# Expert stage of a two-block decoder: the low part of the turned features moved ahead of one weight split

## The reference

```
logits = einsum('nd,de->ne', xt, router_w)
top_val, top_idx = top_k(logits, 2);  gates = softmax(top_val)
for every expert e, on the tokens that chose it:
    y = (silu(xb @ w1[e]) * (xb @ w3[e])) @ w2[e]
out[token] = sum over its two experts of gate * y
```

## Time and profile before

| | |
|---|---|
| time, median of 3 runs | 1962.66 us (1957.55 to 1963.01) |
| the profiled execution's own time | 1963.32 us |
| its span in the profile | 1961.6 us |
| PE busy | 1884.5 us (96%) |
| PE weight loads busy | 1616.9 us (82%) |
| DVE busy | 1542.4 us (79%) |
| ACT busy | 1196.6 us (61%) |
| transfers | 528.39 MB, 269 GB/s over the span |

### The profile page before, as it was taken

The page is one execution under the profiler, slowest core; times in us unless marked ns, Lnnn a source line. Parts: engine busy times, 40 slices in busy tenths (PEclk is TensorE's granted clock), DMA queues, the critical chain, the costliest instruction groups (busy, mean ns, idle before and its releaser), DMA issues.

```text
span 1961.6 us, 27157 instructions
## 1 busy us (share of the span) xinstructions
PE 1884.5 (96%) x10640; PEld 1616.9 (82%) x10640; DVE 1542.4 (79%) x2105; ACT 1196.6 (61%) x1642; POOL 51.3 (3%) x56
## 2 busy tenths in 40 slices
PE   7999999999999999999999999899899989989998
PEld 7889998777878887878787878688789978878997
DVE  5768887567999999999999999558588985856565
ACT  4544344544787888888888887556554446754443
POOL 0010000002000000000000010000000000000000
PEclk9999999999999999999999999999999999999999
DMA  7348886744999999999999999443268974324551
GB/s 311 129 161 308 336 343 248 278 161 156 414 379 377 383 367 380 373 375 367 385 367 388 366 396 360 173 151 108 87 236 331 356 288 151 108 86 166 189 193 44
DMA packets 75901, 528.39 MB, mean 269 GB/s; under 512 B 8658, under 2 KB 9042, under 8 KB 14322
## 3 DMA queue, kind: packets, MB, share of 16 engines
q1 hardware_dynamic: 69536, 504.40, 67.5%
q10 hardware_dynamic: 3060, 11.02, 1.5%
q0 software_dynamic: 3168, 11.14, 1.5%
HBM read 515.90 MB, written 11.01 MB: 269 GB/s over the span
## 4 chain that ended last, share of the span: by engine, by line
PE 87%; DVE 6%; ACT 4%; issue 2%; POOL 1%; DMA 0%; POOLq 0%; ACTq 0%; DVEq 0%
PE ps L554 27%; PE ps L556 26%; PE ps L555 26%; DVE w_lo L1396 2%; PE ps L775 2%; ACT w_hi L2304 1%; PE ps L727 1%; PE ps L740 1%; PE ps L990 1%; POOL stat L2815 1%; ACT xT L2314 0%; PE ps L818 0%; ACT score L2425 0%; ACT y_slots L2608 0%; DMA resid<-in_x 0%
## 5 line engine op out<-in xcount | busy, mean ns | idle before, releaser
L2304 ACT ACTIVATE w_hi<-ring 128x1024 fp32r<-128x1024 f32 x862 | 912.2, 1061 | 603.1 <-PE ps L556 594.7
L1396 DVE TENSOR_TENSOR w_lo<-ring,w_hi 128x1024 fp32r<-128x1024 f32 x862 | 1048.7, 1225 | 284.8 <-ACT w_hi L2304 251.4
L554 PE MATMUL ps<-w_hi,x_hi 128*128 128x512 f32 (+1 forms) x1056 | 410.8, 391 | 8.8 <-DVE w_lo L1396 3.6
L556 PE MATMUL ps<-w_hi,x_lo 128*128 128x512 f32 (+1 forms) x1056 | 400.1, 381 | 0.0
L555 PE MATMUL ps<-w_lo,x_hi 128*128 128x512 f32 (+1 forms) x1056 | 399.1, 380 | 0.0
L554 PE MATMUL ps<-x_hi,w_hi 128*128 128x256 f32 x1248 | 359.6, 288 | 4.6 <-DVE x_lo L1511 3.9
L555 PE MATMUL ps<-x_lo,w_hi 128*128 128x256 f32 x1248 | 355.4, 285 | 0.0
L556 PE MATMUL ps<-x_hi,w_lo 128*128 128x256 f32 x1248 | 355.2, 285 | 0.0
L554 PE MATMUL ps<-w_hi,h_hi 128*128 128x512 f32 x732 | 292.5, 400 | 2.7 <-DVE h_lo L2028 2.6
L555 PE MATMUL ps<-w_lo,h_hi 128*128 128x512 f32 x732 | 285.5, 390 | 0.0
L556 PE MATMUL ps<-w_hi,h_lo 128*128 128x512 f32 x732 | 284.9, 389 | 0.0
(11 more groups left out here) (298 smaller groups left out, 1327.4 us busy)
## 6 DMA issues: line engine op xcount, KB each, us to landing
ring<-in_stream SPq DMA_DIRECT2D x479, 1024.0 KB, 6.6
x_store<-arena ACTq DMA_DIRECT2D x1, 4096.0 KB, 27.5
arena<-x_store POOLq DMA_DIRECT2D x7, 512.0 KB, 8.0
y_store<-y_slots POOLq DMA_DIRECT2D x7, 512.0 KB, 8.9
con<-in_consts ACTq DMA_DIRECT2D x1, 2048.0 KB, 21.4
arena<-in_ln_rows ACTq DMA_DIRECT2D x3, 512.0 KB, 4.3
resid<-in_x SPq DMA_DIRECT2D x1, 1024.0 KB, 6.2
arena<-in_c ACTq DMA_DIRECT2D x2, 512.0 KB, 3.9
```

Of the source, the lines that this page charges most:

```text
L554: pe.matmul(out_, lhs[0], rhs[0], start=start, stop=False)
L556: return pe.matmul(out_, lhs[1], rhs[0], start=False, stop=stop)
L1396: dve.tensor_tensor(lo, ring[:, q % RING, a:a + HALF], hi.bitcast(F32), ALU.subtract)\
L2304: act.activation(half_buffer(m)[0], ring[:, q % RING, a:a + HALF], ACT.Copy).then_inc(hi_ready, 1)
```

## The change

In the order of DVE, `moe_lo` now stands one split earlier in every step s >= 1, as it did in the 11 steps named above. The splits and `moe_lo` are the same instructions with the same waits; ACT, PE, SP and GpSimd have the same programs as before.

```diff
@@ moe_step of the vector engine
                 e, j = s // J1, s % J1
                 n = up_slot(s)
                 if s >= 1:
-                    if j == 9 or (e == NE - 1 and j in (6, 7, 8)):
-                        split_to(reach(2 * n + 1))
-                    else:
-                        split_to(reach(2 * (n + 1)))
+                    split_to(reach(2 * n + 1))
                     moe_lo(s - 1)
                     split_to(reach(2 * (n + 1)))
                 split_to(reach(2 * (n + 2)))
```

## The result

The changed kernel takes 1948.62 us in the median of six runs (1947.48 to 1952.59), the kernel before 1963.01 (1957.55 to 1963.22), six runs beside it. The ratio is 0.9939, 95% interval 0.9928 to 0.995. The profiled execution took 1949.06 us with a span of 1947.3; before it was 1963.32 with 1961.6. Behind line 2052 all lines of the changed kernel lie three lower, so `w_hi` is L2301 and `h_hi` L2596.

The account below looks back on a forecast made before the run. PE was taken as the bound, its weight loads waiting for `h_lo`; 7.1 us (ordinary steps), 3.1 (second steps) and 0.8 (very first) sum to 11.0, taking 1963.32 to 1952.3, by the median 1951.7; predicted 1952, range 1945 to 1960.

Parts of the forecast that it names:

- two large terms: PE's wait for `h_lo` goes: 60 ordinary steps give 7.1 us, seven later second steps (j = 1) 3.1 us.
- the floor: Step length without the wait, 8.44 us, read from a tenth step that already had the new order.
- The alternative by matmul starts: Ordinary steps priced by the up-to-down matmul seam only: 0.54 - 0.45 = 0.09 us each, 5.4 us in all.
- The second term: Seven second steps (j = 1) of the later experts: 0.89 - 0.45 = 0.44 us each, 3.1 us in all.
- The margin at the low part: In step 44 the moved `h_lo` would end 0.9 us before PE needs it.
- D1's split costs nothing: D1's split on DVE comes about 0.7 us later in ordinary steps, with 1.1 us to spare before PE wants it.
- The plug (slower): Rival: DVE holds ready splits behind `h_lo` waiting for `h_hi`, in 76 steps; +17 us, 1980; chance 0.05.
- its point of decision: The plug decides when DVE idles over 0.9 us ahead of `h_lo`, that is, `h_hi` 0.5 us later.
- The transfers: Rival: transfers hold the expert stage, ordinary steps keep their length; only 3.9 us gained, 1959.4; chance 0.11.
- The cover of some 12.5 us: SP's ring: time left from slot issue to ACT's copy, against landings of 7.1 us median, 12.2 at most.

Follow-up runs that it names:

- e2: The changed kernel with the old order left in the second steps (j = 1): 1954.7 us, ratio 0.997.
- e1: The changed kernel with the old order left in the ordinary steps: 1958.11 us, ratio 0.9992.
- e3: The changed kernel with the low part one split earlier still, ahead of D0 and D1: 1986.89 us, ratio 1.014.
- e5: The changed kernel with three linked extra copies by ACT ahead of the real high part, delaying `h_hi`: 1994.81 us, one run.
- e4: The changed kernel with one linked extra copy by ACT ahead of the real high part, delaying `h_hi`: 1954.46 us, ratio 0.9962.
- e6: The changed kernel with slot refills in the expert stage held back until one more slot is split: 1947.7 us, one run.
- e7: The changed kernel with slot refills in the expert stage held back until two more slots are split: 1957.59 us, one run.

## Why the prediction was right

**The size and its two large terms.** For the stage 11.0 us was predicted, 12.0 came, and the experiments split it as the sum did: 7.8 (e2) for the ordinary steps where 7.1 stood, 4.2 (e1) for the second and first steps where 3.9 stood. The small shortfall of the first is the floor: it was read from one tenth step, 8.44, and the freed steps take 8.426, so 0.132 each and not 0.118. The alternative by matmul starts (0.09) would have missed 2.4 us: the whole step was the right measure, since the seam of the two matmuls shows only a part of what the step loses. The second term is by the windows 8.91 - 8.41 = 0.50 rather than 0.44, times seven, and 9.31 - 8.48 = 0.83 for the very first step against the 0.8 taken; these 4.3 agree with e1's 4.2.

**The margin at the low part** was mis-sized, without harm to the sum. "0.9 us before PE needs it" counted to the matmul; the wait stands at the load of its weights and costs from about 0.20 earlier, so the change has 2.79 - 2.04 = 0.75. The same omission made the expectations of e3 and e5 too mild. Neither the prediction nor the change asked whether that wait has to stand there.

**D1's split costs nothing:** shown, 1.17 us to spare up to the matmul where 1.1 was worked out (some 0.2 less up to the load of its weights), and the U1 split back behind ACT.

**The plug (slower).** Rightly given little, but its point of decision was only half understood. The prediction had DVE's idle time decide, from 0.9 us, or `h_hi` 0.5 us later. e4 lies below that (`h_lo` starts 2.05 behind the turn instead of 1.62, 0.76 idle) and is free, e5 and e3 lie above (1.38 and 1.28) and lose. The sum 7.55 + 1.38 = 8.93 even gives e5's step, but that is bookkeeping: DVE's idle time is then all ahead of `h_lo`. What PE waits for there is the low part, and the end of `h_lo` explains the losses of before too, where DVE didn't idle ahead of it at all. By the table the point lies some 0.7 us later (2.79 - 2.04 = 0.75), not 0.5. In e3 D0's split doesn't pass the waiting `h_lo`, though ACT's copy for it is done when `h_lo` starts at 859.25. That agrees with the Trainium skill, "TensorE: Matmul & The Clock Gate", section on the array's architectural detail, which has VectorE work strictly first in, first out. The order tells what is held up, not that it costs: in the changed kernel 0.41 us of waiting a step were free, in e3 0.45 of loss came when a split that PE wants earlier stood behind it.

**The transfers.** The rival falls: 383 GB/s in the ordinary steps of after at the share that gave 377, 409 in the second step. SP's waits and the landing, 470 to 1215 us, changed little against the earlier trace rows:

```profile
SPq L526 <- DVE w_lo L1396: 651.7, 261, 5.1
```

```profile
DMA to landing us min/median/max: 4.8/7.4/12.7
```

The cover of some 12.5 us was right enough for its purpose: e6 takes 2.8 of it at no cost, e7 5.6, and pays. That agrees with a landing of 7.4 in the median and up to 12.7.

**The time as a whole** lies 3.4 us under 1952. 1.0 of that is the stage. The rest is where the runs happen to lie, so that part of the agreement is luck; the range had been made wide for that. In the two profiled executions it is the clock ahead of the stage, and for the other runs no trace shows it.

## What to carry to other kernels

Measure a stage from turn to turn (or any start that repeats) and not by busy time: PE was 42.79 of 42.79 us busy and had 0.13 us a step to give, and 4.2 us that the time couldn't show stood in the stage to a tenth. For an instruction in a strict order, count back from the weight load at which the consumer waits, not from its matmul, ask whether the wait has to stand there, and ask what stands behind it that is wanted before it is done; idle time of an engine with slack is free until then. A step of the same kernel that has the new order already gives the best price for an edit that is to be had without running it.

## What the runs showed of the hardware that was not expected

A wait that stands ahead of the load of a matmul's weights costs nothing until about 0.20 us ahead of the matmul, and then its full lateness: 0.13, 0.46 and 0.51 us lost with the awaited operand done 2.92, 3.24 and 3.30 us behind the turn, where an undelayed matmul starts 2.99 behind it.

An untouched stretch of one program varies by almost 6 us from one execution to the next (first turn at 471.6 to 477.4). Between the profiled executions of before and after, the 3.0 us lie in two places, and in both the granted clock differs: 0.83 against 1.00 from 360 to 370 us, 0.69 against 1.00 in the gather. PE had idled the same 1.68 us ahead of the gather in both, so what lets the clock fall in the one and not in the other stays open.
